# Latent attention's scores from rounded halves in three products, with a reordered beginning and bias tables fetched earlier

## The reference

```python
mod = c_act @ w_ada[l] + b_ada[l]                 # c_act = silu(c); six parts of 1024
h = rms_norm(x, norm1_g) * (1 + sc1) + sh1
# neighbourhood attention: 4 heads of 64
s = where(col_ok, q @ k_band * 64 ** -0.5 + rpb[...], -inf); p = softmax(s); o = p @ v_band
# latent attention: 8 heads, 64 features of their own and 32 rotated ones, key part k_r shared by all heads
s = einsum('bqhd,bkhd->bhqk', q_nope, k_nope) + einsum('bqhr,bkr->bhqk', q_rope, k_r)
p = softmax(s * (64 + 32) ** -0.5);  o = einsum('bhqk,bkhd->bqhd', p, v)
```

## Time and profile before

| | before |
|---|---|
| median of 3 runs | 3087.12 us |
| profiled execution, its own time | 3084.6 us |
| its span, first to last instruction | 3083.0 us |
| PE busy | 2920.8 us (95%) |
| DVE busy | 1776.4 us (58%) |
| ACT busy | 1007.5 us (33%) |
| mean granted TensorE clock | 0.978 |

### The profile page before, as it was taken

How to read it: one execution, slowest core, us unless ns; L and a number is a source line. 1 busy time by engine, 2 the same in 40 slices (tenths; PEclk the granted TensorE clock), 3 DMA queues, 4 the chain that set the end, 5 groups by cost and what they waited for, 6 DMA issues and landing times.

```text
span 3083.0 us, 39822 instructions
## 1 busy us (share of the span) xinstructions
PE 2920.8 (95%) x16215; PEld 2282.2 (74%) x16215; DVE 1776.4 (58%) x1908; ACT 1007.5 (33%) x1307; POOL 429.6 (14%) x464
## 2 busy tenths in 40 slices
PE   2998999999999999999998999999999999999989
PEld 2885666667788888888777888888777876666667
DVE  5556626662445545553487848667654236676783
ACT  2123435552311111111234424334323114454462
POOL 0002010000111111110101103021111002232340
PEclk7999999999999999999999999999999999999999
DMA  6355011011133333331114233243421221212021
GB/s 232 109 171 134 4 28 29 8 29 35 48 103 116 116 116 105 100 101 55 36 48 127 83 89 110 75 137 130 136 104 48 96 96 41 69 35 69 35 74 64
DMA packets 247832, 257.55 MB, mean 84 GB/s; under 512 B 14277, under 2 KB 208674, under 8 KB 247682
## 3 DMA queue, kind: packets, MB, share of 16 engines
q1 hardware_dynamic: 223968, 178.78, 18.9%
q0 software_dynamic: 17680, 58.89, 6.3%
q10 hardware_dynamic: 6034, 17.74, 1.5%
HBM read 222.37 MB, written 30.64 MB: 82 GB/s over the span
## 4 chain that ended last, share of the span: by engine, by line
PE 86%; DVE 8%; ACT 2%; issue 2%; DMA 1%; ACTq 0%; SPq 0%; DVEq 0%
PE PU L994 18%; PE PU L996 18%; PE PU L995 18%; PE PM L1637 2%; PE PU L1615 2%; PE PU L1305 2%; DVE small L2788 2%; PE PM L1657 2%; PE PM L1625 2%; PE PM L1659 2%; PE PM L1658 2%; PE PU L1008 2%; PE PU L1237 1%; PE PU L1009 1%; PE PU L1010 1%
## 5 line engine op out<-in xcount | busy, mean ns | idle before, releaser
L994 PE MATMUL PU<-hH,w_hi_t 128*128 128x512 f32 (+1 forms) x1936 | 764.3, 395 | 4.9 <-DMA hL<-kept_group_low 2.5
L996 PE MATMUL PU<-hH,w_lo_t 128*128 128x512 f32 (+1 forms) x1936 | 755.6, 390 | 0.0
L995 PE MATMUL PU<-hL,w_hi_t 128*128 128x512 f32 (+1 forms) x1936 | 755.0, 390 | 0.0
L994 PEld LDWEIGHTS PU<-hH,w_hi_t 128*128 128x128 f32 (+1 forms) x1936 | 363.4, 188 | 82.6 <-DVE w_lo_t L2380 3.8
L996 PEld LDWEIGHTS PU<-hH,w_lo_t 128*128 128x128 f32 (+1 forms) x1936 | 362.8, 187 | 78.6
L995 PEld LDWEIGHTS PU<-hL,w_hi_t 128*128 128x128 f32 (+1 forms) x1936 | 363.5, 188 | 74.4
L2380 DVE TENSOR_TENSOR w_lo_t<-w_raw,w_hi_t 128x1024 fp32r<-128x1024 f32 x181 | 230.1, 1272 | 301.9 <-ACT w_hi_t L1769 289.8
L1769 ACT ACTIVATE w_hi_t<-w_raw 128x1024 fp32r<-128x1024 f32 x167 | 174.5, 1045 | 440.0 <-PE PU L996 341.0
L2854 DVE SCALAR_TENSOR_TENSOR xT<-PU,mod,xT 128x1024 f32<-128x1024 f32 x120 | 154.0, 1283 | 191.8 <-PE PU L996 191.8
L949 POOL TENSOR_SCALAR_AFFINE_SELECT s_keep<-s_keep 128x128 f32<-128x128 f32 x128 | 114.0, 907 | 504.7 <-ACT s_keep L2268 504.1
L3136 DVE TENSOR_TENSOR_SCAN s_keep<-s_keep,zero 128x128 f32<-128x128 f32 (+7 forms) x128 | 180.6, 1411 | 4.7 <-POOL s_keep L949 4.7
(11 more groups left out here) (417 smaller groups left out, 4836.1 us busy)
## 6 DMA issues: line engine op xcount, KB each, us to landing
ada_w<-in_ada_w_dram POOLq DMA_DIRECT2D x64, 384.0 KB, 4.0
w_raw<-in_w_gu_dram SPq DMA_DIRECT2D x44, 512.0 KB, 3.8
w_raw<-in_m_in_w_dram SPq DMA_DIRECT2D x40, 512.0 KB, 3.9
ada_w<-in_w_ada_dram POOLq DMA_DIRECT2D x32, 512.0 KB, 4.6
seg<-decay_sums SPq DMA_DIRECT2D x32, 512.0 KB, 4.4
w_raw<-in_w_down_dram SPq DMA_DIRECT2D x22, 512.0 KB, 3.4
w_raw<-in_w_in_dram SPq DMA_DIRECT2D x17, 512.0 KB, 3.8
ada_w<-in_w_ada_dram SPq DMA_DIRECT2D x16, 512.0 KB, 18.6
```

The lines of the kernel that those rows point to most:

```text
L994: mm(PU[0:width, up, half, :], whi, aH[:, k, cols], start=k == 0, stop=False)
L995: mm(PU[0:width, up, half, :], whi, aL[:, k, cols], start=False, stop=False)
L996: last = mm(PU[0:width, up, half, :], wlo, aH[:, k, cols], start=False, stop=k == kt - 1)
```

## The change

Three groups of edits.

1. **Scores.** `halves(n)` names 13 operands with their high and low halves: the shared rotated key (`kr`), and for each of four pairs the queries (`q`), keys (`k`) and rotated queries (`r`). `high(n)` on ACT copies into the high half, `low(n)` on DVE subtracts. Four are made ahead of step 0, between and behind the value units; the other nine in steps 2, 5, 6, 11, 12, 14, 17, 19 and 22 (`HALVES_AT`), the low half one step later on DVE. PE waits once for each pair for its halves. The high halves lie in the panel buffers, so that the two output panels which stood there wait until step 27 and until the loop's end.
2. **Beginning.** ACT fetches only `c` and `c_2` (2 DMAs) into `c_stage`; PE transposes that first and `cact` comes from it. POOL issues the other 34 vector DMAs. ACT evicts all 8 tiles of `x`. DVE starts part 0 of the sums as soon as `cact` is there, and copies `vec` and inverts the row root between parts 0 and 1. The write of `bias_rows` moves behind the second slab of the later `w_ada` parts.
3. **Bias tables.** `b2` is two tensors. The first lies where `w_raw` lies and is fetched when the last panel has been split; `na_masked(0)` is the first thing DVE does behind the projection. The folding of `krope`'s squares, the norm of `ckv`, the gains and the second table are spread over the steps (`after_step`).

```diff
-SPLIT_AT = {20: 0, 21: 1, 23: 2, 28: 3}
+SPLIT_AT = {20: 0, 21: 1, 23: 2}
+HALVES = [("kr", 0)] + [(kind, pair) for pair in range(MH // 2) for kind in ("q", "k", "r")]
+HALVES_AT = {2: 4, 5: 5, 6: 6, 11: 7, 12: 8, 14: 9, 17: 10, 19: 11, 22: 12}
 def mla_scores(k):
+    if k % TT == 0:
+        pe.wait_ge(ep_lo, 3 * pair + 4)
+    (_, qh, ql), (_, kh, kl), (_, rh, rl) = (halves(3 * pair + 1 + n) for n in range(3))
     for half in range(2):
-        for hd in range(2):
-            mm(PU[:, hd, half, :], qk[r, 2 * pair, q], qk[r, 2 * pair + 1, half * 512:(half + 1) * 512], ...)
-    for half in range(2):
-        for hd in range(2):
-            last = mm(PU[:, hd, half, :], qr4[pair][r, q], kr4[r, :], start=False, stop=True)
+        for n, (left, right) in enumerate(((qh, kh), (qh, kl), (ql, kh))):
+            for hd in range(2):
+                mm(PU[:, hd, half, :], left[r, q], right[r, cols], start=n == 0, stop=False)
+    for n, (left, right) in enumerate(((rh, kr_hi), (rh, kr_lo), (rl, kr_hi))):
+        for half in range(2):
+            for hd in range(2):
+                last = mm(PU[:, hd, half, :], left[r, q], right[r, :], start=False, stop=n == 2)
+def high(n):                                   # ACT
+    af(dst, src, ACT.Copy).then_inc(ep_hi, 1)
+def low(n):                                    # DVE
+    ve.wait_ge(ep_hi, n + 1)
+    V.tensor_tensor(dst, src, hi.bitcast(F32), ALU.subtract).then_inc(ep_lo, 1)
+if k in HALVES_AT: high(HALVES_AT[k])          # ACT, step k
+if k - 1 in HALVES_AT: low(HALVES_AT[k - 1])   # DVE, step k
-if k == 25: split()
+if k == 27: act.wait_ge(mla_s, 3 * TT); split()
+(after the loop) act.wait_ge(mla_s, MLA_STEPS); split()
 # POOL
+for name, src, ... in VEC_ROWS(a), VEC_PARTS(a): g.dma_start(v_stage[...], src).then_inc(vec_dma, 16)
-g.wait_ge(unit_done[1], len(WIN_UNITS) // 2)
+for p in range(2): g.wait_ge(w_split[p], len(WIN_UNITS) // 2)
+(ahead of the second table) g.wait_ge(unit_done[1], len(WIN_UNITS) // 2)
 # DVE, beginning
 for b in range(2):
+    if b:
+        ve.wait_ge(vec_t, 2)
+        V.tensor_copy(vec[:, :], PM[:, 2, 0:NVEC * P]).then_inc(vec_done, 1)
+        model_inverse()
```

More of the change, by code:

```diff
@@ L1112, in _ @@
                 last.then_inc(x_t, 1)
+            pe.wait_ge(vec_dma, 16 * N_VEC_DMA)
+            for n in range(NVEC):
+                last = nc.tensor.transpose(PM[:, 2, n * P:(n + 1) * P], v_stage[:, n, :], ident[:, :])
+            last.then_inc(vec_t, 1)
+            spread(rt[:, 0, :])
             pe.wait_ge(cact_done, 1)
-            spread(rt[:, 0, :])
+            pe.wait_ge(vec_done, 2)
             for _ in range(2):
@@ L1881, in _ @@
                 if n:
-                    split()
+                    if kind != "krope":
+                        split()
                     if WIN_UNITS[n - 1][0:2] in NORMS:
@@ L1981, in _ @@
                     exp_table()
+                high(n)
             cr.next(HEAD_UNITS)
@@ L2719, in _ @@
                     head_applied((0, 1, 6, 7)[n - 6], n - 6)
+            def low(n):
+                ve.wait_ge(ep_hi, n + 1)
+                src, hi, dst = halves(n)
+                V.tensor_tensor(dst, src, hi.bitcast(F32), ALU.subtract).then_inc(ep_lo, 1)
             head_applied(8, 4)
             head_applied(9, 5)
+            for n in range(4):
+                low(n)
             cr.next(HEAD_UNITS)
```

207 lines of the change are left out of this document (128 added, 79 removed).

## The result

| | before | changed |
|---|---|---|
| median | 3087.60 us (3082.66 to 3091.01) | 3049.69 us (3045.74 to 3052.48) |
| profiled execution | 3084.6 us | 3049.4 us |
| its span | 3083.0 us | 3047.7 us |
| PE busy | 2920.8 us | 2901.2 us |

The ratio is 0.9875, with a 95% interval of 0.9859 to 0.9891. Predicted were 3048 us, a ratio of 0.9873. So the change makes the kernel 1.0 to 1.3% faster by these two measurements, and the forecast lies at the faster end of that.

The account below looks back on a forecast made before the run. PE's time and its idle places were taken as the bound (86% of the chain). Beginning -17.1, neighbourhood attention -11.2 and latent loop -10.8 sum to -39.1 against 3084.6: 3045.5, plus 2.5 for the median, 3048 us; range 3031 to 3066.

Parts of the forecast that it names:

- the 1.0 us charged for them: Beginning: part 1 waits for vectors from POOL's 34 issues, there at 32.5 us against 31.5 for part 0's end.
- Rival 1: Beginning: POOL's vector rows come late and put part 1 at 44 us; adds 12, 3060 us; chance 0.15.
- The slow clock: Neighbourhood attention, steps 1 to 8: matmuls slower after PE's long idle time; half of 5.3 us goes, -2.7.
- The calculation with the overhead kept: Latent loop scores: 9 waves of 0.2265 us plus an unchanged 0.41 of changing over, 2.45 us.
- rival 2: Latent loop: scores save nothing, issue or weight loads bind at about 3.0 us; adds 18.6, 3066 us; chance 0.13.
- rival 4: Latent loop: rounded matmuls of different row groups don't run side by side; scores 5.85 us, total 3158; chance 0.03.
- Rival 3: Latent loop overhead goes, scores at 2.10 us, and all of the slow clock goes; 3035 us; chance 0.12.
- Entry: Latent loop, before step 0: ACT's high(3) and DVE's low(3) now delay the first scores, +2.3 us.
- steps 8, 16 and 24: Latent loop: each new pair waits for the low half of its rotated queries, +1.8, +0.5 and +1.8 us.
- The overfull ACT: Latent loop: a split behind the root step in step 21 and a panel in step 27, +0.7 us each.
- The cover at the end: Loop's end: second output panel split while PE makes the last two steps' values, 0; without it 1 to 2 us.
- rival 5: Early table or early sums wait for something else, only one of two gains comes; about 3060 us; chance 0.07.

Follow-up runs that it names:

- e5: Changed kernel, but DVE copies the vectors and inverts the row root ahead of the first part of the sums, as before; 3060.39 us, ratio 0.9915.
- e6: Changed kernel, but the folding of krope's squares and the ckv norm stand ahead of the first bias table again; 3059.21 us, ratio 0.9916.
- e2: Changed kernel, but PE waits for the halves of the rotated queries just ahead of the products that read them; 3042.42 us, ratio 0.9859.
- e4: Changed kernel without the products of the queries' low half, rotated ones too: two products instead of three; 3028.31 us, one run.
- e8: Changed kernel with e2's later waits, e7's w_ada order, moved output-panel halves and split, vectors and root copied within part two; 3037.73 us, ratio 0.9852.
- e12: The kernel of e2 measured once more, unaltered; 3044.07 us, ratio 0.9860.
- e9: Changed kernel, but both heads' products of queries and keys read the same rows, 0 to 63; 3119.65 us, one run.
- e1: Changed kernel with the float32 scores of before put back and no halves made; 3057.75 us, ratio 0.9917.
- e11: Changed kernel measured again on another chip with nothing altered; 3052.26 us, ratio 0.9899.
- e3: Changed kernel with the three products of a head queued together instead of alternating heads; 3058.86 us, one run.
- e10: Changed kernel with all six products of queries and keys of one head queued before the other head's six; 3084.52 us, one run.
- e7: Changed kernel, but SP asks for the eight blocks of w_ada's first part ahead of x; 3055.36 us, ratio 0.9892.

## Why the prediction was right, step by step

**Beginning, -17.1 predicted, -16.9 measured.** The mechanism is as told. e5 shows 7.6 us of it; the other 9.3 are read from the traces. Two terms were off and cancelled, which is luck. Part 0 starts at 19.97, not 18.5, and ends at 32.9, not 31.5. POOL's issues of single rows take 0.50 us on average (34 from 4.75 to 21.8), not 0.65, and land in 5.0, not 6, so the vectors are turned at 26.9 and not 32.5, and the 1.0 us charged for them falls away. Rival 1 was never near: 6 us of slack. The group of these issues in the changed kernel:

```profile
L838 POOL DMA_DIRECT2D v_stage<-in_mla_qr_g_dram x4: 487/487/487, 17.9 to 20.9; - x4
...
DMA to landing us min/median/max: 4.9/5.0/5.5
```

**Neighbourhood attention, -11.2 predicted, -12.9 measured.** The first bias row gained 10.5 (10.4 predicted: from 13.0 to 2.5 us between the scores of steps 0 and 1). The moved work costs 2.6 us more of waiting instead of 1.9: behind the first wait PE waits 3.6 us for DVE's rows and 1.7 for ACT, where it waited 2.1 and 0.6. The slow clock went altogether in this profile, 5.0 us of PE's busy time in the steps 1 to 8, where I had taken half of 5.3. The term that was mis-sized is that half. I had no row to say how much of the low clock belonged to the wait; e6 shows that the 4 us behind the wait do. In four of the later profiles (e2, e4, e8, e12) the stage has the clock low for some 3 us and is 1.2 to 1.3 us longer, so that they give -11.6 to -11.7.

**Scores, -0.58 a step predicted, -0.51 measured.** 2.50 us instead of 2.41, and 6.85 us a step instead of 6.80. The calculation with the overhead kept, 9 waves of 0.2265 and 0.41, gave 2.45 and was the better one; I had averaged it with one in which the overhead shrinks with the work. e4 measures both parts: a wave is 0.23, the overhead 0.41 to 0.43. The 0.07 us a step between forecast and measurement are 2.2 us of the sum over the loop. That PE keeps up with 24 matmuls and 24 weight loads (rival 2) and that the heads run side by side in the rounded type (rival 4) is shown by every step, and by e9 why. Rival 3's 2.10 did not come: the overhead stays. Of the Trainium skill, TensorE: Matmul & The Clock Gate, I had cited 3.07 for four row tiles (Part 3, Measured speedup vs the span model): twelve such matmuls take 0.90 us here (500.85 to 501.75), 12 x 0.2265 / 0.90 = 3.0, and the trace agrees. The 62 ns a matmul that its section "Wait — 56ns, not 53.3ns?" gives for the sequencer without hardware decode do not show: four groups start every 0.23 us, 57 to 58 ns a matmul.

**Added work in the loop.** Entry +2.3 predicted, +2.3 measured; steps 8, 16 and 24 +1.8, +0.5, +1.8 predicted, +1.83, +0.56, +1.83 measured (8.67, 8.67 and 8.68 us, where a regular step has 6.85 and a step with the 8 small matmuls 8.11). e2 and e12 show that all of it is PE's wait and avoidable (6.2 of the 6.5 us came back, the rest is clock in the first steps). The overfull ACT: predicted 0.7 behind steps 21 and 27, measured 0.48 and 0.49, one step later each, since the delay comes through the exponentials of the next step. The cover at the end held: the output projection starts without a wait. The loop and its entry gave -9.2 (the table's +2.3 and -11.5) where -10.8 was predicted, and e1 confirms it with 8.7.

**The sum.** -39.1 predicted; -40.0 at the start of the output projection, -35.3 at the end of the span. The 4.7 between are scatter (e11, e12). My 2.5 us from profile to median are 3.0 for the kernel before (3087.60, with a fourth run) and 0.3 for the changed one. So the total came within 2 us partly by luck: neighbourhood attention gave 1.7 us more and the loop 1.6 less, and the 4.7 us lost behind the loop meet 2.2 that the median did not add and 0.9 more than forecast ahead of it. The mechanisms do not rest on that: each stretch moved as told, and both the early table and the early sums gave their gain, so that rival 5 fell.

**What the prediction left out.** That PE can be at the lower clock behind a longer wait, which I had used for neighbourhood attention and not for the entry that I had just made longer, from 1.11 to 3.41 us: 1 to 4 us there in five of six profiles with the same products (0.50 to 0.69 over the first 5 us), and 1.5 to 2.6 more in the steps 8, 16 and 24 together.

## What to carry to other kernels

Where an operand is late, wait for it just ahead of the product that reads it and put the other products first: the change lost 6.2 us to waits that stood ahead of products which did not need the operand, and e2 gets them back. Small-row matmuls of different row groups run together in rounded float32 as they do in float32, and PE finds the partner past two or three matmuls that have to wait (e3, e10). Count waves, not matmuls, and measure what the changes of group add: 0.4 us a step here. A long idle stretch of a queue is filled best by what needs the fewest inputs, but look at what the next engine needs by then (e7).

## What the runs showed of the hardware

- Matmuls on other rows overtake. In e10 the seventh in the queue starts at 509.15, ahead of the fourth to sixth. The Trainium skill, TensorE: Matmul & The Clock Gate, Part 3 (The mechanism), has weight loads pulled ahead and says that matmuls start and end strictly in order. By that rule the seventh would start no earlier than the sixth, so that e10 would need eleven waves where it has eight, 0.7 us more a step than the 7.41 measured, and e3 nine where it has six; the traces do not agree.
- The loops whose products of queries and keys use one half of the rows, throughout (e9) or in part (e10), were granted a lower clock, 0.87 and 0.90 over 311 and 276 us, against 0.95 to 0.99 in the same loop with the halves together, though PE was no less busy (96% and 95% against 93%). These are two executions only, both behind a wait of 3.41 us, so the cause is open.
- The granted clock at the loop's entry goes with the wait ahead of it: 1.00 over the first 5 us of scores behind 1.11 us of waiting in five of five profiles, 0.50 to 0.69 behind 3.41 us in eight of nine.
- Two executions of one kernel that agree within 0.1 us over the first 652 us (e2, e12) end 8.7 us apart. A difference below that between single profiles is read from the stage that was edited, not from the span.
